# Head norms of a two-block transformer kernel: the root mean square in columns of 128 tokens by 2 heads, its factor spread back by TensorE

## What is computed

```python
def rms_norm(x, g):
    xf = x.astype(jnp.float32)
    y = xf * lax.rsqrt(jnp.mean(xf * xf, axis=-1, keepdims=True) + RMS_EPS)
    return (y * g.astype(jnp.float32)).astype(x.dtype)

def even_mixer(u, uc, w_in, w_four, q_g, k_g, rpb, w_out, update_ctx):
    p = u @ w_in
    f, q, k, v = jnp.split(p, [FOUR_WIDTH, FOUR_WIDTH + NA_WIDTH, FOUR_WIDTH + 2 * NA_WIDTH], axis=-1)
    q = rms_norm(split_heads(q), q_g)
    k = rms_norm(split_heads(k), k_g)
    ...
    kc = rms_norm(split_heads(kc), k_g)
    ...
    o_four = fourier_mix(f, w_four)
    o_na = neighbourhood_attention(q, k, v, kc, vc, rpb)
```

## Time and profile before

| | us |
|---|---|
| median of 3 runs | 2247.85 |
| lowest and highest | 2245.47, 2248.17 |
| span of the profiled execution, first to last instruction | 2244.5 |
| TensorE busy | 2097.8 (93%) |
| VectorE busy | 972.6 (43%) |
| ScalarE busy | 684.9 (31%) |
| GpSimd busy | 793.6 (35%) |

### The profile page before, as it was taken

One profiled execution on the slowest core, in us unless ns is written; L12 is line 12 of the kernel. 1 busy time (PEld: TensorE's weight loads), 2 busy tenths in 40 slices (PEclk: granted clock), 3 DMA queues, 4 the chain that ended last, 5 costly groups with the idle time before them and its releaser, 6 DMA issues. The chain is left out here.

```text
span 2244.5 us, 25972 instructions
## 1 busy us (share of the span) xinstructions
PE 2097.8 (93%) x10180; PEld 1690.7 (75%) x10180; DVE 972.6 (43%) x1696; ACT 684.9 (31%) x912; POOL 793.6 (35%) x240
## 2 busy tenths in 40 slices
PE   7998998799999979999998979999996998999998
PEld 3876576587878867888886747888885876888886
DVE  1575469677595735233142281014444123312122
ACT  2322352222122233222123373245543233222122
POOL 2322123344444443444444203442321443444444
PEclk9899999799999979999999999999997999999999
DMA  8163004242352232222222102222120222222221
GB/s 344 44 239 80 1 32 173 115 188 112 150 224 111 100 124 75 94 93 95 106 98 81 57 1 93 94 75 76 57 76 19 97 91 76 94 94 99 105 77 38
DMA packets 42773, 224.25 MB, mean 100 GB/s; under 512 B 12736, under 2 KB 13248, under 8 KB 17216
## 3 DMA queue, kind: packets, MB, share of 16 engines
q1 hardware_dynamic: 42688, 223.08, 27.4%
HBM read 218.86 MB, written 2.10 MB: 98 GB/s over the span
## 5 line engine op out<-in xcount | busy, mean ns | idle before, releaser
L815 POOL TENSOR_TENSOR wl<-raw,wh 128x2048 fp32r<-128x2048 f32 (+1 forms) x155 | 710.9, 4587 | 1279.0 <-ACT wh L461 1279.0
L896 PE MATMUL bank<-uh,wh 128*128 128x512 f32 x1480 | 592.4, 400 | 31.4 <-POOL wl L815 7.3
L897 PE MATMUL bank<-ul,wh 128*128 128x512 f32 x1480 | 583.9, 394 | 0.0
L898 PE MATMUL bank<-uh,wl 128*128 128x512 f32 x1480 | 583.6, 394 | 0.0
L461 ACT ACTIVATE wh<-raw 128x2048 fp32r<-128x2048 f32 (+1 forms) x155 | 292.8, 1889 | 601.6 <-PE bank L898 588.7
L896 PEld LDWEIGHTS bank<-uh,wh 128*128 128x128 f32 x1480 | 283.2, 191 | 98.5 <-issue 27.2
L896 PE MATMUL bank<-ah,wh 128*128 128x512 f32 x816 | 322.8, 396 | 6.4 <-DVE al L1720 6.4
L898 PEld LDWEIGHTS bank<-uh,wl 128*128 128x128 f32 x1480 | 282.5, 191 | 60.7
L897 PEld LDWEIGHTS bank<-ul,wh 128*128 128x128 f32 x1480 | 283.2, 191 | 58.9 <-issue 1.0
L898 PE MATMUL bank<-ah,wl 128*128 128x512 f32 x816 | 320.6, 393 | 0.0
L897 PE MATMUL bank<-al,wh 128*128 128x512 f32 x816 | 317.7, 389 | 0.0
(11 more groups left out here) (211 smaller groups left out, 2100.2 us busy)
## 6 DMA issues: line engine op xcount, KB each, us to landing
raw<-in_w SPq DMA_DIRECT2D x64, 1024.0 KB, 6.7
mraw<-in_w_modr SPq DMA_DIRECT2D x40, 1024.0 KB, 4.9
raw<-in_w_gu SPq DMA_DIRECT2D x22, 1024.0 KB, 4.9
raw<-in_w_hg SPq DMA_DIRECT2D x16, 1024.0 KB, 4.9
modf<-in_w_modf SPq DMA_DIRECT2D x8, 1024.0 KB, 17.8
raw<-in_w_in SPq DMA_DIRECT2D x8, 1024.0 KB, 17.8
raw<-in_w_out SPq DMA_DIRECT2D x8, 1024.0 KB, 6.0
raw<-in_w_dn SPq DMA_DIRECT2D x8, 1024.0 KB, 4.9
```

The costliest lines, as they stand in the source:

```text
L815: pool.tensor_tensor(wl[:, b % 2, 0:nk], raw[:, b % RAW, 0:nk], f32(wh[:, b % 2, 0:nk]), ALU.subtract).then_inc(split_lo, 1)
L896: pe.matmul(out, ah_, bh, start=first, stop=False)
L897: pe.matmul(out, ah_, bl, start=False, stop=False)
L898: return pe.matmul(out, al_, bh, start=False, stop=last)
```

## The change

The mean squares are no longer spread over the partitions by the sum itself. The square tile is now the weight operand, 128 tokens at a time, and the moving operand is two columns of `ones_h`; the result is 128 tokens by 2 heads, four times, 8 columns in all. Root and reciprocal work on these 8 columns (`hst`). TensorE then spreads the factor back: for each of 4 groups of tokens and 2 heads it takes the column, repeated 64 times, as weights, and the identity as the moving operand (`head_spread`, 8 products a unit, into bank 4). ScalarE copies the projection with the gain out of PSUM into `tt` (`hn_copy`), which frees the bank, and VectorE multiplies copy and spread factor (`hn_scale`).

Unit i is spread one point later than its sum, in front of sum i + 1; the last one behind (7, 1). The order of the units changes too: both context tiles come early, since bank 4 is now used by the spreads.

```diff
-        HN = [("k", 0), ("k", 1), ("kc", 0), ("k", 2), ("k", 3), ("q", 0), ("q", 1), ("q", 2), ("q", 3), ("kc", 1)]
+        HN = [("kc", 0), ("k", 0), ("k", 1), ("kc", 1), ("k", 2), ("k", 3), ("q", 0), ("q", 1), ("q", 2), ("q", 3)]
...
+            def hn_copy(i):
+
+                src, free, _ = hn_place(i)
+                if i >= 2:
+                    act.wait_ge(hn_done, i - 1)
+                gain = vec[:, V_QG:V_QG + 1] if HN[i][0] == "q" else vec[:, V_KG:V_KG + 1]
+                act.activation(tt[:, i % 2], src, ACT.Copy, scale=gain).then_inc(free, 1)
...
-                    act.activation(tt[:, i % 2], bank[6][:], ACT.Sqrt, bias=eps_col).then_inc(hroot_ready, 1)
+                    act.activation(hst[:, 0, i % 2, :], hn_sums(i), ACT.Sqrt, bias=eps_col).then_inc(hroot_ready, 1)
...
                             hn_root(i)
+                            if i + 1 < len(HN):
+                                hn_copy(i + 1)
                             if i + 2 < len(HN):
                                 hn_square(i + 2)
...
-                pe.matmul(bank[6][:], ones_h, sq[:, i % 2], start=True, stop=True).then_inc(hsum_full, 1)
+                for a in range(4):
+                    last = pe.matmul(hn_sums(i)[:, 2 * a:2 * a + 2], sq[:, i % 2, P * a:P * a + P], ones_h, start=True, stop=True)
+                last.then_inc(hsum_full, 1)
+
+            def head_spread(i):
+                pe.wait_ge(hrstd_ready, i + 1)
+                if i:
+                    pe.wait_ge(hn_done, i)
+                else:
+                    pe.wait_ge(ctx_free, 3)
+                for a in range(4):
+                    for e in range(2):
+                        last = pe.matmul(bank[4][DH * e:DH * e + DH, P * a:P * a + P], hst[:, 1, i % 2, 2 * a + e:2 * a + e + 1].to_broadcast([P, DH]), ident, start=True, stop=True)
+                last.then_inc(hbc_full, 1)
...
                     if (b, half) in HN_AFTER:
-                        head_sum(HN_AFTER[b, half])
+                        i = HN_AFTER[b, half]
+                        if i:
+                            head_spread(i - 1)
+                        head_sum(i)
+                    if (b, half) == (7, 1):
+                        head_spread(len(HN) - 1)
...
             pe.wait_ge(ctx_free, 4)
+            pe.wait_ge(hn_done, len(HN))
...
+            def hn_invert(i):
+
+                dve.wait_ge(hroot_ready, i + 1)
+                if i >= 2:
+                    dve.wait_ge(hbc_full, i - 1)
+                dve.reciprocal(hst[:, 1, i % 2, :], hst[:, 0, i % 2, :]).then_inc(hrstd_ready, 1)
...
+                hn_wait_copied(dve, i)
+                dve.wait_ge(hbc_full, i + 1)
...
+                dve.tensor_tensor(out, x, r, ALU.mult).then_inc(hn_done, 1)
```

More of the change, by code:

```diff
@@ L92, in build_program @@
         rc = at("rc", [P, 2, 4], F32, o); o += 32
+        hst = at("hst", [P, 2, 2, 8], F32, o); o += 128
         A = (o + 31) // 32 * 32
@@ L193, in build_program @@
             sem("v_copied"), sem("vwin_in"), sem("tab_in"), sem("dft_in"), sem("w4_in"))
-        hsq_ready, hsum_full, hroot_ready, hrstd_ready, hn_done = (
-            sem("hsq_ready"), sem("hsum_full"), sem("hroot_ready"), sem("hrstd_ready"), sem("hn_done"))
+        hsq_ready, hsum_full, hroot_ready, hrstd_ready, hbc_full, hn_done = (
+            sem("hsq_ready"), sem("hsum_full"), sem("hroot_ready"), sem("hrstd_ready"), sem("hbc_full"), sem("hn_done"))
         f_copied, cw_full, cw_ready, y_full, y_ready, four_full, four_hi, four_lo = (
@@ L226, in build_program @@
         ones_d = con[:, C_OND:C_OND + P]
-        ones_h = con[:, C_ONH:C_ONH + P]
+        ones_h = con[:, C_ONH:C_ONH + P:DH]
         ones_v = con[:, C_ONV:C_ONV + P]
@@ L279, in hn_wait, with hn_sums, hn_wait_copied @@
                 eng.wait_ge(bank_full[bank_of(b, m % 2)], used(b) + 1)
-        def hn_wait_done(eng, i):
+        def hn_sums(i):
+            return bank[6][:, 8 * (i % 2):8 * (i % 2) + 8]
+        def hn_wait_copied(eng, i):
             kind, m = HN[i]
@@ L510, in hn_root @@
                 if i >= 2:
-                    hn_wait_done(act, i - 2)
+                    act.wait_ge(hrstd_ready, i - 1)
                 if HN[i][0] == "q":
-                    act.activation(tt[:, i % 2], bank[6][:], ACT.Sqrt, bias=epsq_col, scale=float(DH)).then_inc(hroot_ready, 1)
+                    act.activation(hst[:, 0, i % 2, :], hn_sums(i), ACT.Sqrt, bias=epsq_col, scale=float(DH)).then_inc(hroot_ready, 1)
                 else:
-                    act.activation(tt[:, i % 2], bank[6][:], ACT.Sqrt, bias=eps_col).then_inc(hroot_ready, 1)
+                    act.activation(hst[:, 0, i % 2, :], hn_sums(i), ACT.Sqrt, bias=eps_col).then_inc(hroot_ready, 1)
             for b in range(8):
@@ L524, in _ @@
                     hn_square(0)
+                    hn_copy(0)
                     hn_square(1)
@@ L1057, in scores @@
                     pe.wait_ge(four_lo, 3 + i)
-                    for n in range(len(HN)):
-                        hn_wait_done(pe, n)
+                    pe.wait_ge(hn_done, len(HN))
                 else:
@@ L1415, in _ @@
             norm("ctx", ctxT, lambda k: gm[:, 1, k:k + 1], lambda k: modx[:, k:k + 1], uch, ucl, L)
-            def hn_scale(i):
[L1419 to L1429, removed]
+            def hn_invert(i):
[3 more added lines that the diff above has]
+                dve.reciprocal(hst[:, 1, i % 2, :], hst[:, 0, i % 2, :]).then_inc(hrstd_ready, 1)
+            def hn_scale(i):
+                hn_wait_copied(dve, i)
+                dve.wait_ge(hbc_full, i + 1)
+                out, x, r = hn_place(i)[2], tt[:, i % 2], bank[4][:]
+                if HN[i][0] == "q":
+                    out = out.rearrange("p (w r c) -> p w r c", r=ROWS, c=QC)
+                    x, r = (y.rearrange("p (r w c) -> p w r c", w=QT, c=QC) for y in (x, r))
+                dve.tensor_tensor(out, x, r, ALU.mult).then_inc(hn_done, 1)
             mod_sum(0)
@@ L1439, in _ @@
                     if (b, half) in HN_AFTER:
-                        hn_scale(HN_AFTER[b, half])
+                        i = HN_AFTER[b, half]
+                        if i:
+                            hn_scale(i - 1)
+                        hn_invert(i)
+                    if (b, half) == (7, 1):
+                        hn_scale(len(HN) - 1)
                     if half == 0 and b + 1 < PROJ:
```

## The result

The changed kernel takes 2256.79 us (median of 6 runs), the kernel before 2246.59 us beside it. The ratio is 1.0037, with an interval from 1.0025 to 1.005: slower by about a third of a per cent, 8 to 9 us. That is inside the range (2243.4 to 2256.9), close to its upper end, but outside "same", which had the largest chance. Nearly all of the loss arises after the stage that was forecast, in code that the change did not touch.

The account below looks back on a forecast made before the run. TensorE, busy 93% of the span, bounds the kernel; VectorE's lateness makes it wait in the norms. -13.5 (waits, clock) + 12.0 (spreads) + 0 (sums) + 1.5 + 0.6 (added waits) = +0.6 us: 2248.4 us, range 2243.4 to 2256.9.

Parts of the forecast that it names:

- The bound and the two waits: At 130 to 204 us VectorE is full; TensorE's bank waits of 4.82 and 4.43 us go, -13.5 us with the low clock.
- The low clock: TensorE at 1.2 GHz in place of 2.4 behind the two bank waits, costing 1.95 + 2.33 = 4.28 us, would go.
- (e): As forecast, but with the low clock after the wait at 130 us: 2250.5 us; with the forecast 67%.
- The sign that I went by: After a lone TensorE wait of 2.92 us the next pass took 0.50 us, full speed; so no low clock at 130 us.
- The spreads: Ten new spreads of 16 passes on TensorE, 1.2 us each after neighbour L1254: +12.0 us, bounds +8.7 and +20.5.
- the upper bound: A TensorE spread with no overlap at all: 16 x 0.11 + 0.3 = 2.05 us, +20.5 us for ten.
- rival (b): Weight loads lie bare between the spreads' passes: 3.5 us or more a spread, 2271 us; 3%.
- The sums: Ten column sums on TensorE, now eight passes each, at 0.86 us as before: no difference, 0.1 us either way each.
- The added waits: TensorE waits for inversion 0 near 130 us, +1.5 us, and the Fourier weights' products wait for product 9, +0.6 us.
- the sign by which it would be wrong: A difference that arises after 204 us, where nothing was changed, would show the forecast wrong.
- rival (a): Column halves do not overlap in the spreads: 2.05 us each, 8.5 us more in all, 2256.9 us; 13%.

Follow-up runs that it names:

- the two kernels with waits of 1.84 and 1.30 us: The changed kernel with the new tile hst behind all others, ratio 0.9995 to before; and the changed kernel with A 64 bytes higher, ratio 0.9985.
- the changed kernel moved by 64: The changed kernel with everything from A on 64 bytes higher, 192 above the kernel before: 2243.86 us, ratio 0.9985 to the kernel before.
- The kernel with one column half: Changed kernel moved 64 bytes, inversion 0 ahead of modulation sum 3, all eight products of a spread in one column half (wrong results): 2250.88 us, one run.
- the kernel with the early release alone: Kernel before with A 192 bytes higher; ScalarE copies projection times gain out of PSUM behind its square, no spreads, reciprocals stay 128x512: 2237.91 us, ratio 0.9952 to before.

## Why the prediction came out as it did

**The bound and the two waits** held. They are gone, with 9.25 us of standing still, and VectorE's share fell. Its busy time is 23.0 us and not 35: I had left the modulation sums as they were, and these too fell, from 25.8 us in the stretch (L1386 and L1389) to 15.3 (L1420 and L1423). Before, some of their steps ran beside GpSimd's splits of the weights, as the 4.42 us step at 139.40; in the changed kernel none does, and the first steps come out at 0.30 us instead of 1.60 on average, the others at 0.49 instead of 0.63. That was worth nothing on TensorE.

**The low clock** I took as gone with both waits, and kept its return behind the wait at 130 us for (e). In the profile of the changed kernel it did return: the half block behind the wait runs from 133.10 to 140.32, 7.22 us instead of 5.56. In the two kernels with waits of 1.84 and 1.30 us it did not, and the clock of 130 to 204 us is 1.00 in both. So (e) came true in one of three traces, at 1.7 us. The sign that I went by, full speed after a lone wait of 2.92 us, doesn't carry: at the same place in the changed kernel moved by 64 a shorter wait was followed by the low clock, with 0.79 us for the first pass and five of 0.63 us behind it:

```profile
1218.54 0.79 PE L912 MATMUL bank<-uh,wh 128*128 128x512 f32 x1 [2.42 <-POOL wl L831]
```

The length of a wait alone doesn't decide whether the clock falls; what does is open.

**The spreads** held: 1.03 us to the next group and some 0.1 ahead of it, against 1.2. This was the deciding term, and L1254 the right neighbour for it. The kernel with one column half took 1.89 us, close to the 2.05 of the upper bound, and rival (b)'s 3.5 us is far off. The rule of the Trainium skill (TensorE: Matmul & The Clock Gate, Part 3) that stood behind (b), that weight loads overlap only where row groups differ, isn't what the 16 passes in 1.03 us show, nor the 16 in one column half, which follow each other at 0.118 us, about as close as L1086's.

**The sums** were 0.05 us dearer each, not equal: 131.71 to 132.62 is 0.91 us against 0.86. Ten are +0.5, inside the 0.1 either way.

**The added waits** were 0.97 (1.30 and 1.84 in two other builds) for 1.5, and 0.41 for 0.6.

In all: -13.5 + 11.5 (ten spreads at 1.15) + 0.5 + 0.97 + 0.41 + 1.66 (the clock) = +1.5, less 0.3 because TensorE reached the point at 129.71 instead of 130.03: +1.2 against 1.07 measured. The forecast was +0.6. One reading beside the sum was off and changed nothing: the 3.35 us by which the median lay above the profiled span are not all start and end; in every run on record time and span differ by 1.7 to 1.9 us, and the rest is scatter between executions.

**Between 205 and 405 us** the changed kernel gained 3 us that no term had: it stands 1.07 behind at the first and 1.99 ahead at the second. The table of stretches shows two places with a higher clock. Before:

```profile
250.00:266.00 16.00, 15.76 (x64) 11.09 (x64) 8.60 (x25) 6.71 (x15) 3.63 (x5) 0.68 0.01 2
342.00:402.00 60.00, 50.98 (x220) 41.77 (x218) 48.39 (x78) 11.52 (x12) 23.89 (x10) 0.89 0.52 193
```

After:

```profile
250.00:266.00 16.00, 14.83 (x68) 10.43 (x69) 9.91 (x29) 7.42 (x17) 4.32 (x6) 0.79 0.00 1
342.00:402.00 60.00, 49.06 (x223) 40.52 (x221) 46.82 (x78) 11.78 (x13) 22.78 (x10) 0.92 0.53 193
```

The two other kernels with the whole change and the wait at 130 us gained there too (3.2 and 3.0 us), while the five builds of the kernel before with moved tiles took between 0.2 us more and 1.8 us less for it than the kernel before. Why the clock is higher in unchanged code isn't settled. With it the account closes: 1.07 - 3.06 + 10.5 = 8.5 us, against the 8.80 by which the last `diag` product is late.

**The step that failed** is not a term of the sum but one that is missing: the sum treats the new tile as free, and no rival has it. Its declaration was not in the diff as I cut it, and I took "nothing was changed after 204 us" for granted. 128 bytes in front of the large tiles changed the distance of 2448 passes by 0.0043 us each, 10.5 us. The prediction named the sign by which it would be wrong, a difference that arises after 204 us, and that is what came. Had I added the term, I still could not have given its size: in the trace of before, passes over `ah` stand at 0.2290 and those over `uh` at 0.227, and this difference of 0.002 us was the only trace of it. That the time fell inside the range all the same is luck: its upper end was set for rival (a), whose mechanism did not occur, and the 10.5 us of passes happened to be of a like size.

## What to carry to other kernels

When a change adds a tile, see which tiles it moves, and compare the distance between passes of the same kind before and after in a stage that the change doesn't touch; here a difference of 2% there was worth 10.5 us, and the change itself nothing that could be measured. When TensorE waits for a bank that a slow engine reads last, first let any engine copy it out, and see whether that alone is enough before the slow work is made smaller with products on the engine that is the bound. When a trade is to be judged, give both kernels the same addresses first.

## What the runs showed of the hardware

**The distance between fp32r passes depends on where the moving tile lies relative to the weights**: 0.2267 us where the tiles are a multiple of 256 bytes apart, 0.2290 to 0.2343 at the other five remainders that were tried, up to 3.4% more. Moving all tiles together changed nothing. That the remainder by 256 is the right measure is read off seven values; that it is the weights' load that gets in the way of the moving operand's reading is an inference, and no run separates it from another tile at the same distance. The Trainium skill says (TensorE: Matmul & The Clock Gate, Part 2) that the weights and the moving operand have read ports of their own, so that a load takes nothing from a running product. No run here measures the ports, but a distance that changes with where the tiles lie relative to each other, in kernels whose instructions are the same, is hard to square with a load that takes nothing.

**Some steps of VectorE that read only SBUF grow several times longer beside a GpSimd operation.** VectorE in the kernel with the early release alone:

```profile
138.93 0.69 DVE L1434 TENSOR_TENSOR kT<-kT,tt 128x512 f32<-128x512 f32 x1
139.53 4.69 DVE L1393 TENSOR_SCALAR acc<-mraw,csil 128x256 f32<-128x256 f32 x1
...
155.22 2.35 DVE L1434 TENSOR_TENSOR kT<-kT,tt 128x512 f32<-128x512 f32 x1
157.50 0.34 DVE L1393 TENSOR_SCALAR acc<-mraw,csil 128x256 f32<-128x256 f32 x1
```

GpSimd in the same kernel:

```profile
139.31 4.77 POOL L823 TENSOR_TENSOR wl<-raw,wh 128x2048 fp32r<-128x2048 f32 x1 [13.25 <-ACT wh L464]
152.43 4.61 POOL L823 TENSOR_TENSOR wl<-raw,wh 128x2048 fp32r<-128x2048 f32 x1 [8.35 <-ACT wh L464]
```

The same step takes 0.34 us alone and 4.69 beside the split from 139.31 on; the same product 0.69 alone and 2.35 while the split from 152.43 to 157.04 runs. Each ends just behind the split, 0.1 and 0.5 us after it. The reciprocal from 151.85 on, beside the second split, took 3.34 us as always. Products that read one input from PSUM were not held up: those of line L1492 before took 0.69 us each, and 12 of the 32 ran beside a GpSimd operation. The ten of the changed kernel took 688 ns, but none of them ran beside a split.
